# A bias table in another buffer, the first half's front in another order, and one projection for the compressed keys and values of both groups

## What is computed

```
mod = silu(c) @ w_mod + b_mod                      # six vectors of 1024: sh1, sc1, gt1, sh2, sc2, gt2
h   = rmsnorm(x) * (1 + sc1) + sh1
q, kc, vc, ks, vs, kw, vw, gates, cb, cc, ch = split(h @ w_in)
# attention, 8 heads of 64 in 2 groups; three branches, weighed by sigmoid(gates):
kc, vc = gelu(flat(blocks of 32 tokens, stride 16, + pe) @ w1) @ w2      # per group: 15 compressed keys, values
p = softmax(q k^T * scale + rel_table[bucket(distance)])                # for kc, ks and kw
o_conv = cb * conv3(cc * ch)
x  = x + gt1 * (concat(rmsnorm(o_attn), rmsnorm(o_conv)) @ w_out)
h2 = rmsnorm(x) * (1 + sc2) + sh2
# peer: 8 heads, top 16 of 128*128 experts each by product keys, so 128 experts per token
x  = x + gt2 * sum_e softmax(score)_e * gelu(h2 . u[e]) * v[e]
```

## Time and profile before

| what | us |
|---|---|
| median of three runs (1430.6 to 1432.1) | 1430.66 |
| the profiled execution | 1434.69 |
| its span | 1432.9 |
| PE busy in the span | 1162.1 (81%) |
| DVE busy | 744.8 (52%) |
| ACT busy | 487.7 (34%) |
| POOL busy | 362.8 (25%) |

### The profile page before, as it was taken

One profiled execution on the slowest core, in us unless ns is written; L12 is line 12 of the kernel. 1 busy time (PEld: TensorE's weight loads), 2 busy tenths in 40 slices (PEclk: granted clock), 3 DMA queues, 4 the chain that ended last, 5 costly groups with the idle time before them and its releaser, 6 DMA issues.

```text
span 1432.9 us, 15094 instructions
## 1 busy us (share of the span) xinstructions
PE 1162.1 (81%) x5592; PEld 676.0 (47%) x5592; DVE 744.8 (52%) x1811; ACT 487.7 (34%) x1284; POOL 362.8 (25%) x285
## 2 busy tenths in 40 slices
PE   5999885868877776666677776669998998999997
PEld 2688563422422232111122221124777887899883
DVE  4213468768859974455544445440266566642102
ACT  1022124453434332334333333321477553212201
POOL 0878202243334432334333434300000000000000
PEclk8998886889988998999899889889998999999999
DMA  9863505789999999999999999924431321114130
GB/s 362 315 250 148 219 1 215 298 327 422 400 421 420 409 374 395 421 422 421 422 400 402 386 394 422 422 121 178 176 118 59 118 103 75 61 60 177 59 118 30
DMA packets 56853, 377.59 MB, mean 264 GB/s; under 512 B 7139, under 2 KB 10380, under 8 KB 11916
## 3 DMA queue, kind: packets, MB, share of 16 engines
q0 software_dynamic: 36864, 268.45, 45.9%
q1 hardware_dynamic: 19248, 106.13, 19.2%
q10 hardware_dynamic: 668, 2.04, 0.4%
HBM read 375.54 MB, written 1.06 MB: 263 GB/s over the span
## 4 chain that ended last, share of the span: by engine, by line
PE 53%; DMA 20%; DVE 15%; ACT 8%; issue 2%; POOL 1%; ACTq 0%; POOLq 0%; DVEq 0%
PE ps L88 53%; DMA AR<-in_puv,idx 19%; DVE AR L88 8%; DVE RT L88 3%; ACT L88 2%; ACT av L88 2%; DVE rowb L88 1%; ACT acc L88 1%; POOL AR L88 1%; DVE acc L88 1%; ACT rowb L88 1%; DMA scr<-tok 1%; ACT AR L88 1%; DVE junk L88 1%; DVE tok L88 0%
## 5 line engine op out<-in xcount | busy, mean ns | idle before, releaser
L88 PE MATMUL ps<-AR,acc 128*64 128x512 f32 x960 | 372.8, 700 | 183.5 <-ACT acc L88 182.1
L88 POOL DMA_INDIRECT AR<-in_puv,idx x256 | 270.3, 1056 | 512.4 <-PE ps L88 405.6
L88 PE MATMUL ps<-hT,W 128*128 128x256 f32 (+2 forms) x1504 | 324.9, 375 | 5.5 <-ACT rowb L88 3.0
L88 PEld LDWEIGHTS ps<-AR,acc 128*64 128x64 f32 x960 | 92.3, 151 | 436.6 <-ACT acc L88 351.3
L88 PEld LDWEIGHTS ps<-hT,W 128*128 128x128 f32 (+1 forms) x1504 | 271.0, 196 | 57.1 <-issue 14.5
L88 DVE CUSTOM_DVE_ANT_0 AR<-AR,mixT 128x1024 f32<-128x1024 f32 x128 | 156.8, 1227 | 156.7 <-DMA AR<-in_puv,idx 156.5
L88 DVE CUSTOM_DVE_ANT_0 AR<-AR,tok 128x1024 f32<-128x1024 f32 x128 | 153.0, 1220 | 62.2 <-DMA AR<-in_puv,idx 62.0
L88 ACT ACTIVATE av<-av 128x1 f32<-128x1 f32 x256 | 51.3, 200 | 305.2 <-DVE av L88 305.1
L88 ACT ACT_TABLE_LOAD x106 | 136.0, 1283 | 12.5 <-DVE tok L88 10.7
L88 PE MATMUL ps<-W,hT 128*128 128x512 f32 (+3 forms) x288 | 97.7, 497 | 0.8 <-ACT hT L88 0.8
L88 ACT ACTIVATE acc<-fold,av 128x64 f32<-128x64 f32 x240 | 83.5, 348 | 7.9
(11 more groups left out here) (230 smaller groups left out, 1084.6 us busy)
## 6 DMA issues: line engine op xcount, KB each, us to landing
W<-in_w_in SPq DMA_DIRECT2D x50, 1024.0 KB, 6.8
W<-in_w_mod SPq DMA_DIRECT2D x24, 1024.0 KB, 11.1
W<-in_w_out SPq DMA_DIRECT2D x4, 1024.0 KB, 5.8
W<-in_wq SPq DMA_DIRECT2D x4, 1024.0 KB, 9.9
AR<-in_puv,idx POOLq DMA_INDIRECT x256
W<-in_wba SPq DMA_DIRECT2D x4, 1024.0 KB, 5.9
W<-in_wbb SPq DMA_DIRECT2D x4, 1024.0 KB, 5.9
W<-in_wo SPq DMA_DIRECT2D x4, 1024.0 KB, 6.0
```

The source lines that it names most:

```text
L88: ins = f(*args, **kw)
```

## The change

- The one-hot rows, the table and `fh` move from `tok2` to `PT`, which is first written by `turn_p(0)`; `norm_x` then waits for nothing of them.
- The modulation sums of POOL go to `RT` and to free rows of `rowb` in place of `junk` and `mixT`, so they no longer wait for `t_B`; `flip_bias` is moved from before to after the projection of kc, vc, ks and vs.
- `cw`, the compression's weights, is loaded twice, once for each 64 partitions, in four DMAs. The projections of kc and vc make all 128 rows (both groups) at once; `blk` holds the groups on partitions 0 to 63 and 64 to 127; `compress` issues for each of the 32 taps two matmuls, one for each group, on 15 columns.
- In the front of half 0, `conv_step(0, 0)` and `conv_step(1, 0)` go into the projection loop, with `weigh(3)` between them; `pv_(3)` and `attn_root(0)` come first, and the Square in `attn_root` doesn't wait for the row sums any more; `mod_cols_sum` comes after `attn_mm(0, 1)`; a matmul of `attn_mm` waits for its own slice of `mixT` (`t_mk`).
- Unit 4: `scores_mm(4)` goes behind `q_norm`, `scores_add(4)` ahead of `route`; `weigh(4)`, `turn_p(4)`, `pv_(4)` and all of unit 5 go into `half1`, which becomes two steps longer. The 29 pieces of `route` ahead of p = 0 go; after each combine there are 10 (p < 3), 5 (p < 14) and then 8.

```diff
-        oh_sb = tok2[0:33, 0, 0:383]
-        tab = tok2[0:33, 1, 0:8]
+        PT = sb("PT", [P, 2, 1024])
+        oh_sb = PT[0:33, 0, 0:383]
+        tab = PT[0:33, 1, 0:8]
...
-        fh = tok2[0:8, 1, 16:399]
+        fh = PT[0:8, 1, 16:399]
...
-        t_xb = [norm_x(a, st[:, 8 + a:9 + a], [t_x], tok2, [t_ohfree, t_scr]) for a in range(2)]
+        t_xb = [norm_x(a, st[:, 8 + a:9 + a], [t_x], tok2, []) for a in range(2)]
...
-        t_cw = SP.dma(nc.sync.dma_start, s_cw, cw, cmpw)
+        for g in range(2):
+            for c in (0, 2144):
+                t_cw = SP.dma(nc.sync.dma_start, s_cw, cw[g * 64:g * 64 + 64, c:c + 2144], cmpw[:, c:c + 2144])
...
-            for g in range(2):
-                t = feat(w, col(v * 128 + g * 64, 64), hT, t_w, t_h, b, g * 256, 64)
...
+            t = feat(w, col(v * 128), hT, t_w, t_h, b, 0)
...
-                t = PE(mm, b.t[0:64, 0:30], cw[:, 64 + v * 2048 + q * 64:64 + v * 2048 + q * 64 + 64],
-                       blk[:, v, q, :, :].rearrange("p g n -> p (g n)"), start=(q == 0), stop=(q == 31),
-                       after=b.old + t_blk[v] + [t_cw])
+                for g in range(2):
+                    r = slice(g * 64, g * 64 + 64)
+                    t = PE(mm, b.t[r, 0:15], cw[r, 64 + v * 2048 + q * 64:64 + v * 2048 + q * 64 + 64], blk[r, v, q, :],
+                           start=(q == 0), stop=(q == 31), after=b.old + t_blk[v] + [t_cw])
...
                 run_step(2)
+                if (n, j2) == (2, 0):
+                    conv_step(0, 0)
+                    weigh(3)
+                    conv_step(1, 0)
...
-                       after=b.old + [t_w] + t_mix[a])
+                       after=b.old + [t_w, t_mk[a][k]])
...
-        advance(routes[0], 29)
-        scores_add(5)
...
+            yield [lambda: weigh(4), lambda: scores_mm(5)]
+            yield [lambda: scores_add(5), lambda: turn_p(4)]
+            yield [lambda: weigh(5), lambda: pv_(4), lambda: scores_mm(6)]
...
-            advance(routes[0], 4 if p < 12 else 8)
+            advance(routes[0], 10 if p < 3 else 5 if p < 14 else 8)
```

More of the change, by code:

```diff
@@ L404, in build @@
         t_ms = []
+        ms_buf = [RT[:, 512 * n:512 * n + 512] for n in range(3)] + [R_POST[:, 0:512], R_POST[:, 512:1024], R_LNF[:, 0:512]]
         def mod_next():
             n = len(t_ms)
[L408 to L413, removed]
+            t_ms.append((ms_buf[n], mod_sum(ms_buf[n], [])))
         i, w, t_w = next_w()
@@ L453, in build @@
         mod_next()
+        t_B = flip_bias()
         i, w, t_w = next_w()
@@ L511, in compress_v @@
         def compress_v():
-            b = ps.take()
+            bs = [ps.take(), ps.take()]
             for g in range(2):
[L514 to L517, removed]
+                r = slice(g * 64, g * 64 + 64)
+                t = PE(mm, bs[g].t[0:15, 0:64], zcmp[r, 1, 0:15], cw[r, 64 + 4160:64 + 4224], start=True, stop=True,
+                       after=bs[g].old + [t_gel[1]])
+            for g in range(2):
+                t_c["v"] = V(cpv, vc[0:15, g * 64:g * 64 + 64], bs[g].t[0:15, 0:64], after=[t])
+                bs[g].free = [t_c["v"]]
         O = [ps.take(), ps.take()]
@@ L662, in build, with conv_step @@
                   lambda: (cmp_turn(0, 0), cmp_turn(0, 1)),
-                  lambda: (cmp_add(0, 0), cmp_add(0, 1), pv_(0), pv_(1), turn_p(2), scores(3), weigh(3)),
+                  lambda: (cmp_add(0, 0), cmp_add(0, 1), pv_(0), pv_(1), turn_p(2), scores(3)),
                   ]
+        def conv_step(j, a):
+            c0, c = a * P, slice(a * P, a * P + P)
+            wc = [PV[:, V_CW + r * 4 + j:V_CW + r * 4 + j + 1] for r in range(3)]
+            o = oc[:, j, c]
+            t = V(ts_, o, z[:, j, c0:c0 + P], wc[0], None, MUL, after=[t_cv[2, j // 2], t_zz])
+            t = V(stt, o, z[:, j, c0 + 1:c0 + 1 + P], wc[1], o, MUL, ADD, after=[t])
+            t = V(stt, o, z[:, j, c0 + 2:c0 + 2 + P], wc[2], o, MUL, ADD, after=[t])
+            t = V(tt_, o, o, cbT[:, j, c], MUL, after=[t, t_cv[0, j // 2]])
+            t_oc[a].append(V(tt_, cbT[:, j, c], o, o, MUL, after=[t]))
         oc = ccT
+        t_oc = [[], []]
         t_zz = G(nc.gpsimd.memset, z[:, :, 0:2], 0.0)
@@ L1035, in build @@
         attn_add(0, 0)
-        scores(4)
         attn_mm(0, 1)
-        weigh(4)
+        b2 = ps.take()
+        for n in range(4):
+            t_mc.append(mod_cols_sum(b2, 4 * n, *t_ms[n]))
         attn_add(0, 1)
-        turn_p(4)
         norm_root(("c", 1), nrm[:, 1, :], cbT[:, :, P:2 * P], t_oc[1])
-        q_norm(0, [])
+        q_norm1(0)
+        sh2, sc2, t_m2 = mod_affine(b2, t_mc[3], 24, V_LNF, 16)
+        q_norm2(0, [])
+        scores_mm(4)
         q_project(0, 0)
```

82 lines of the change are left out of this document (33 added, 49 removed).

## The result

| | before | changed |
|---|---|---|
| median, us | 1430.63 (4 runs, 1429.89 to 1432.1) | 1414.33 (4 runs, 1411.04 to 1418.85) |
| ratio, 95% interval | | 0.9887 [0.9858, 0.9916] |
| the profiled execution, us | 1434.69 | 1413.83 |
| its span, us | 1432.9 | 1412.0 |

The median fell by 16.3 us, the span by 20.9. The changed kernel's four runs scatter over 7.8 us and those of before over 2.2, but in the four later sittings those of the kernel before scatter over 7.2 to 14.7, so this is no mark of the change.

A forecast was written before the change was run, and what follows sets the result against it. PE bounds the projections, order and engine chains the front, DMA the gathers from 301.7 us. Terms -3.5 - 7.0 + 0 - 11.8 + 4 = -18.3 us gave 1416.4 profiled, 1412.4 median; range 1402 to 1424.

The forecast's parts named there:

- Bias table: At the start, the first normed half no longer waits for the table's way to DRAM: 3.5 us gained, lower bound 0.
- kc and vc: In the projections, 32 instructions with 128 output rows replace 64 with 64 rows: 7.0 us less.
- compress: In the compression, twice the matmuls on half the columns, about 30 ns each at full clock: 0, bounds 0 and +11.
- cw and flip_bias: In the projections, longer loading of cw on SP may delay kw's slab: costs 0 to 4 us, taken as 0.
- Front: Front of half 0, projections' end to first gather: w_out and q_project start earlier, 11.8 us gained, bounds 8 and 15.
- the step had 3.1: Front, between w_out and q_project: q_norm waiting for PE costs 2.4 us, scores_mm(4) another 0.7.
- The 1.5 for q_project: Front: one PE idle gap fewer before q_project, so half the difference between 6.75 and 3.84 us is gained.
- Start of the gathers: First gathers: earlier first release, but two more steps and more routing pieces: 4 us lost, bounds 5 gained to 12 lost.
- the pairs are not serial: Denies the rival for the compression: paired matmuls run serially, gain falls to 7.3 us, 1423.4; chance 0.08.
- starving buffers: Rival at the first ten gather steps: five buffers starve the stream, about 9 us slower, 1440; chance 0.07.
- the start used up in part: Rival: late weights, lower clock, SP holding kw's slab or 9 us steps leave 0 to 7 us, about 1427; chance 0.09.

The follow-up runs named there:

- x6_29ahead: Changed kernel with 29 routing pieces ahead of the first gather step and four after each combine up to step 13; 1406.39 us, ratio 0.9839.
- n7_root_later: Changed kernel with the root of half 1's convolution moved behind half 0's query norm; 1406.98 us, ratio 0.9863.
- The turned order: Changed kernel with the compression's matmuls reordered, all 32 taps of group 0, then all of group 1; 1426.55 us, ratio 0.9951.
- n9_taps_spread: Changed kernel with the compression's small matmuls in five pieces behind projections instead of two runs; 1412.66 us, ratio 0.9877.
- x4_banks: Changed kernel with the two groups of each compression in PSUM banks of their own; 1413.16 us (one run).

## Why the prediction was right

*Bias table: -3.5 expected, -4.9 at the begin of q (-3.9 in the second profile of the changed kernel).* The mechanism held (first half at 17.07). In the first profile PE's wait for DVE's part of the sums shrank too (4.03 to 1.41), and the 16 matmuls behind that wait took 5.30 in place of 6.35. Undone it cost 4.0 and 4.6 at that place. With the table alone undone and POOL kept out of the way, 3.1 of it are left at the first gather against x6_29ahead, and 2 to 3 in the median; that all of it reaches the end is not shown.

*kc and vc: -7.0 expected, projections 5.4 shorter.* The instructions did what the step says: the first 112 of the changed kernel take 24.41 us, 0.218 each. The rest is the two rows behind, 14.24 + 9.14 = 23.4 us before and 25.0 now; the half clock began 4.5 us into the first of them and lasted 13.6 (102.4 to 116.0), now 3.7 and 17.1. The view of stretches of the kernel before, inside that:

```profile
102.40:115.40 13.00, 13.00 (x88) 12.02 (x87) 5.41 (x7) 5.64 (x13) 12.77 (x5) 0.50 0.30 122
```

I had left the clock as it was. The 1.6 lost in these rows are not a price of the change, though: x6_29ahead and n7_root_later have the same code up to there, and in their profiles the half clock lasts 13.7, as before, and the projections take 106.85 and 106.39 us, 6.9 and 7.3 less than before. So the -7.0 was right, and the 5.4 is that of a profile with a longer half clock.

*compress: 0 expected, 0.6 measured* on the row with both runs (14.24 to 14.88; 13.9 to 15.1 over the profiles with the changed order). The turned order costs 13.25 us, so the pairs overlap. At full clock 64 of their rows take 2.04 us in n9_taps_spread, 32 ns each where the step has 30. The Trainium skill (TensorEngine Tiling (Array Packing), Restrictions and Gotchas) says that different row tiles cannot access one bank at once. The prediction put the price of that at 11 us; x4_banks shows 14.73 us with two banks against 14.88 with one. The measurement decides: no run here shows that rule.

*cw and flip_bias: 0 expected.* SP was held for 11.03 us, DVE stood idle for 27.03 us until cw had come, and PE lost 0.16 at one slab:

```profile
37.27 11.03 SPq L88 DMA_DIRECT2D AR<-in_cmpw  x4
```

```profile
66.19 1.35 DVE L88 TENSOR_TENSOR AR<-ps,AR 128x240 f32<-128x240 f32 x4 [27.03 <-DMA AR<-in_cmpw]
```

*Front: -11.8 expected, -10.9 measured.* w_out begins 7.1 us after the projections' end, 12.0 sooner than the 19.1 of before (11.4 expected). The two groups take 13.90 where 8.75 + 7.13 stood, a gain of 2.0 that the sum did not have. From w_out's end to q_project it is 13.3 in place of 6.7, 6.6 lost where the step had 3.1: the rows before q_project ran at half clock, and 3.78 for scores(4) beside 1.99 and 1.94 for the transposes beside 1.09 are 2.6 of the missing 3.5. This term is the one that was mis-sized; the 2.0 in w_out and the earlier start hid most of it. n7_root_later gives 3.0 to 4.4 back. The 1.5 for q_project came as 1.6 (5.19 in place of 6.75), by luck as much as by reason: its rows still began at half clock, and other profiles have 4.98 to 5.96. From the first matmul behind q_project on, both kernels take 11.66.

*Start of the gathers: +4 expected, +2.4 by the 26th gather.* The first release was sooner than I had it (13.6, not 16.4), as the first dot began 5.6 us after the first gather, on one expert's data, and not 8. Ten steps then took 79.0, where 75 + 3.9 was written. The sign of the loss held, and its size within a factor of two; x6_29ahead shows that its cause, pieces of `route` in the steps, is avoidable and worth 7.7.

The sum was -18.3; the span gave -20.9 and the medians -16.3. Two errors met: the stages gave 2.6 more than I wrote, and the profile of the changed kernel lay closer to its median than that of before. That the median came within 2 us of 1412.4 is therefore luck in part; what held are the terms, stage by stage. Of the rivals none came: the pairs are not serial, and the mean step was 7.9, below the 9.8 from which starving buffers would have decided. Of the third, the start used up in part, only the lower clock behind w_out is there.

## What to carry to other kernels

A wait of one engine at a start of transfers is room for work that would otherwise stand in later steps; move it there before making the first transfer a few us earlier. Before comparing the length of a stage that fills PE in two profiles, read the granted clock of both: here equal code had 13.7 us at half clock in one profile and 17.1 in another, and that alone made a saving of 7 us look like 5.4, and a cost of 3 look like none. And when a small DVE instruction takes several us, look at what POOL ends at that moment.

## What was not expected of the hardware

*DVE behind POOL.* An instruction of 0.17 us took 6.01 and ended with POOL's product to within 0.02 us; with POOL ordered behind it, it took 0.17. The Trainium skill (SBUF — State Buffer, Who interferes with whom) says that a DVE instruction with two inputs in SBUF blocks against a GpSimd one that reads SBUF, and that the second to issue waits for the whole of the first. The traces agree: 41.89 + 6.01 = 47.90 beside 40.87 + 7.01 = 47.88. In the kernel before, the same instruction, which follows the last one of the earlier trace rows, began at 41.90, and POOL's product at 42.05: 0.15 us kept it from a wait of some 6. The same stands elsewhere in both kernels, where PE had other work: a DVE product on 128x4, also with both inputs in SBUF and 0.17 us long when alone, takes 5.50 us in the kernel before and ends at 141.79 beside POOL's 141.78, and 5.79 in the changed kernel, at 96.34 beside 96.31.

*Half clock without a pause.* In the changed kernel PE was busy for all of 86.0 to 106.8, and the clock fell to 0.50, its lower level of 1.2 GHz, at 89.7, 3.7 us after the first row with small matmuls. With the same instructions in five pieces between projections it stayed at 1.00 over the pieces in all three profiles of such kernels, and in all eleven with two runs it fell. How long it then stays down differs between executions of equal code, as 13.7 and 17.1 us show.
